# Attention values in one visit per step, three turned-weight banks, and the output-weight split on GpSimd

## The chip, the cores and the metric

The kernel runs on one core of a Trainium2 chip. The metric is the device time of one execution in microseconds (us), as the median of repeated runs. Beside it there is one profiled execution, whose trace all rows below come from.

## The reference

One inference step of a one-layer encoder, all in fp32. 1024 prompt tokens and 64 sample tokens (which also see a cache of 2048 positions) go through RMSNorm and one input projection of 3072 columns, then through two mixers side by side, an output matrix, a SwiGLU block and a final norm.

```python
qd, kd, vd, qs, ks_, vs = _project(n, w_in[l])
# differential attention: 4 heads, two 64-wide maps each, values 128 wide
p = softmax(where(visible, q.k/8 - slope*dist, -1e30))
a = p[:, :, 0] - lam * p[:, :, 1];  o = a @ v
# stick-breaking attention: 8 heads of 64, strictly causal
z = q.k/8;  log_keep = where(causal, log_sigmoid(-z), 0)
a = where(causal, exp(log_sigmoid(z) + cumsum_from_the_right(log_keep) - log_keep), 0);  o = a @ v
hp = xp + concat(od, osb) @ w_out[l]
y = rms_norm(hp + swiglu(hp, ...))
```

## The kernel before

The program goes through the projection, then `attend` (both attentions), then `mix` (the output matrix), then the feed-forward block. The change is in `attend` alone.

**Steps.** `attend` has 8 units (`NU`): 4 differential heads (`ND`), then 4 pairs of stick-breaking heads. A unit has 5 steps (`SPU`): four prompt steps of two query blocks each (1152 key columns together, for two maps or two heads), and one sample step of 2112 columns. So there are 40 steps; 0 to 19 are differential, 20 to 39 (`SB0` on) stick-breaking.

**One iteration, written by hand.** All engines run the same loop over iterations -3 to 40 and each iteration has three slices (`SLICES`, slots 0 and 1, slots 2 and 3, slot 4). In iteration i, slice by slice, TensorE does:

- `turn`: it transposes groups of the finished weights z of step i (3 groups for a differential prompt step, 5 for the others) into a bank of `ps_aT` (L1776);
- `values`: it multiplies turned weights, copied by ScalarE from `ps_aT` to `aT` (`collect`, L1445), with the values into `ps_o` (L1802, L1809, L1805);
- `score`: the products q.k of step i+3, up to 512 columns a unit, into the ring of four banks `ps_z` (L1743 to L1760);
- `prepare`: transposes of raw keys for the next unit, also through the ring (L1722). ScalarE and VectorE split them into a high and a low part (L1397, L1524).

A score or a prepare waits in `release` until the bank that it takes has been read. In the differential half VectorE reads the scores (`read_scores`, L1575) and ScalarE then takes the exponentials (`exps`, L1419); VectorE joins the two maps (`combine`, L1602). In the stick-breaking half ScalarE reads the scores with a sigmoid (`keep`, L1431 and L1436) and VectorE runs a scan over them (`survive`, L1619). A differential prompt score takes two banks a unit, one for each map; a sample score takes one.

**Where values stand.** `LAG` is 2. A differential step's group has its values at the slot of the group two places further on, so a prompt step has one group in the second slice of its own iteration and two in the first slice of the next. A stick-breaking step up to 37 (`gathered`) has four groups in the third slice of its own iteration and the fifth in that of the next. `ps_aT` has 2 banks, `ps_o` 2, `aT` 6 places.

**The output matrix's split.** VectorE splits w_out into a rounded high part (`split_w_out`, L1642) and the rest (`low_w_out`, L1649), 16 pieces of 128x512, at the ends of iterations 21 to 36. SyncE loads the pieces into the ring of six raw places `staging`, which the raw keys and values use too, in one fixed order, and waits for the release of the piece six places before. GpSimd multiplies `lowest` by a slope once per differential step (L1355), builds the masks, and is then idle until `mix`.

## Time and profile before

| what | value |
|---|---|
| median of 3 runs | 1408.41 us (1406.29 to 1408.46) |
| profiled execution | 1405.33 us, of which the span is 1403.5 us |
| TensorE busy | 1357.6 us, 97% |
| VectorE busy | 998.1 us, 71% |
| ScalarE busy | 620.5 us, 44% |
| GpSimd busy | 453.8 us, 32% |
| `attend` | from about 277 us to 575.9 us |
| iterations 20 to 39 of it | 434.9 us to the last scan's end, 571.8 us |

Busy time counts an instruction from its start to its end, with any time that it stands still in between. Matmuls overlap, so TensorE's gaps are best seen at its weight loads (PEld): each matmul has one, and "[0.29 <-X]" behind a row is the time that the engine stood idle before it and what ended that.

### The profile page before, as it was taken

Reading aid. Unit: us, or ns where it says so; the run is one execution under the profiler, and the core shown is the slowest. Engines: PE = TensorE matmul, PEld = TensorE weight load, DVE = VectorE, ACT = ScalarE, POOL = GpSimd, SP = SyncE. Lnnn points to the kernel's source line nnn. Section 1 sums busy time; section 2 is a strip of 40 time slices with the busy share of each in tenths; the row PEclk is TensorE's granted clock in tenths of the full one; section 3 lists DMA queues with packets and bytes.
Section 4 is the critical chain, followed back from the end, with each engine's and each line's share of the span. In section 5 each row is a group of like instructions: output and inputs, shape, how many; then the busy total and the mean of one; then the engine's idle time right before and its main releaser. Section 6 shows DMA issues by size and latency. Waiting matters only on the chain.

```text
span 1403.5 us, 23797 instructions
## 1 busy us (share of the span) xinstructions
PE 1357.6 (97%) x9152; PEld 1194.3 (85%) x9152; DVE 998.1 (71%) x1317; ACT 620.5 (44%) x1112; POOL 453.8 (32%) x416
## 2 busy tenths in 40 slices
PE   6999999989999999999799999999999999999997
PEld 5778888768888787788689999999999998788886
DVE  5896858698868999766686766565766666753466
ACT  6634333278887877333342132232132233533343
POOL 2133331200010000111274454454454454644354
PEclk9999999999999999999999999999999999999999
DMA  7265542465444555433134443444443448855554
GB/s 250 76 213 187 204 160 74 145 174 142 129 128 116 143 140 144 149 136 108 54 121 154 165 156 109 145 145 153 167 154 110 147 173 288 298 175 165 164 181 172
DMA packets 172200, 218.05 MB, mean 155 GB/s; under 512 B 19836, under 2 KB 110328, under 8 KB 170680
## 3 DMA queue, kind: packets, MB, share of 16 engines
q1 hardware_dynamic: 163416, 193.13, 42.5%
q0 software_dynamic: 3840, 12.58, 2.8%
q10 hardware_dynamic: 4832, 10.82, 2.1%
q8 instruction: 74, 1.21, 0.4%
q14 instruction: 38, 0.31, 0.1%
HBM read 152.98 MB, written 63.50 MB: 154 GB/s over the span
## 4 chain that ended last, share of the span: by engine, by line
PE 47%; DVE 1%; DMA 1%; issue 1%; ACT 0%; SPq 0%; POOL 0%; ACTq 0%; DVEq 0%
PE ps_feed L2997 11%; PE ps_feed L2998 11%; PE ps_feed L2999 11%; PE ps_feed L3028 4%; PE ps_feed L3027 4%; PE ps_feed L3026 4%; PE ps_feed L3042 1%; PE ps_feed L3043 1%; DMA aux<-in_w_down 1%; DMA aux<-t_dram 0%; DVE parts_early L2865 0%; DVE shared L2865 0%; DVE blocks L2843 0%; DVE blocks L2844 0%; DVE blocks L2910 0%
## 5 line engine op out<-in xcount | busy, mean ns | idle before, releaser
L792 PE MATMUL ps_proj<-shared 128*128 128x512 f32 x224 | 90.1, 402 | 2.1 <-DVE shared L546 1.2
L2678 ACT COPY aux<-ps_feed 128x544 f32<-128x544 f32 x22 | 13.5, 615 | 170.3 <-PE ps_feed L2999 170.3
L1445 ACT COPY aT<-ps_aT 128x512 f32<-128x512 f32 (+2 forms) x168 | 81.4, 528 | 16.7 <-PE ps_aT L1776 16.2
L793 PE MATMUL ps_proj<-shared 128*128 128x512 f32 x224 | 88.3, 394 | 0.0
L794 PE MATMUL ps_proj<-shared 128*128 128x512 f32 x224 | 88.1, 393 | 0.0
L2628 POOL TENSOR_TENSOR ring_more<-staging,ring_more 128x512 fp32r<-128x512 f32 x45 | 69.6, 1550 | 56.5 <-ACT ring_more L2664 56.3
L2628 POOL TENSOR_TENSOR shared<-staging,shared 128x512 fp32r<-128x512 f32 x41 | 60.0, 1468 | 83.4 <-ACT shared L2664 83.4
L1776 PE MATMUL ps_aT<-ident,z 128*128 128x128 f32 (+1 forms) x568 | 82.7, 279 | 3.4 <-DVE z L1619 2.1
L2892 DVE TENSOR_TENSOR blocks<-ps_feed,blocks 128x512 f32<-128x512 f32 x56 | 36.0, 682 | 66.2 <-PE ps_feed L3028 66.2
L1619 DVE TENSOR_TENSOR_SCAN z<-z,near 128x1024 f32<-128x1024 f32 (+7 forms) x64 | 81.4, 1334 | 0.0
L2997 PE MATMUL ps_feed<-shared,ring_more 128*128 128x272 f32 x264 | 76.6, 290 | 1.8 <-issue 1.8
L2997 PE MATMUL ps_feed<-parts_early,shared 128*128 128x272 f32 x256 | 74.5, 291 | 2.7 <-PEq L3184 2.7
L2999 PE MATMUL ps_feed<-shared,ring_more 128*128 128x272 f32 x264 | 76.2, 289 | 0.0
L1776 PEld LDWEIGHTS ps_aT<-ident,z 128*128 128x128 f32 (+1 forms) x568 | 63.3, 141 | 15.1 <-issue 7.4
L2998 PE MATMUL ps_feed<-shared 128*128 128x272 f32 x264 | 76.1, 288 | 0.0
L2998 PE MATMUL ps_feed<-parts_early,ring_more 128*128 128x272 f32 x264 | 76.1, 288 | 0.0
L2999 PE MATMUL ps_feed<-shared 128*128 128x272 f32 x264 | 76.1, 288 | 0.0
L2998 PE MATMUL ps_feed<-shared,ring_more 128*128 128x272 f32 x264 | 76.1, 288 | 0.0
L2999 PE MATMUL ps_feed<-parts_early,ring_more 128*128 128x272 f32 x264 | 76.0, 288 | 0.0
L2997 PE MATMUL ps_feed<-parts_early,ring_more 128*128 128x272 f32 x264 | 76.0, 288 | 0.0
L2997 PE MATMUL ps_feed<-shared 128*128 128x272 f32 x264 | 75.6, 286 | 0.0
L2998 PE MATMUL ps_feed<-parts_early,shared 128*128 128x272 f32 x256 | 74.6, 291 | 0.0
(372 smaller groups left out, 4520.3 us busy)
## 6 DMA issues: line engine op xcount, KB each, us to landing
staging<-s_dram SPq DMA_DIRECT2D x50, 256.0 KB, 4.4
staging<-in_w_gate SPq DMA_DIRECT2D x11, 1024.0 KB, 7.8
blocks<-in_w_up SPq DMA_DIRECT2D x11, 1024.0 KB, 5.4
blocks<-in_w_down SPq DMA_DIRECT2D x11, 1024.0 KB, 9.8
t_dram<-blocks SPq DMA_DIRECT2D x11, 1024.0 KB, 3.9
s_dram<-blocks SPq DMA_DIRECT2D x11, 1024.0 KB, 5.2
w_raw<-in_w_in SPq DMA_DIRECT2D x10, 1024.0 KB, 6.6
staging<-in_cache_sb_v POOLq DMA_DIRECT2D x31, 256.0 KB, 3.2
```

The source lines that it names most:

```text
L792: nc.tensor.matmul(res, a_hi[:, k, cols], b_hi[:, k], start=start, stop=False)
L793: nc.tensor.matmul(res, a_hi[:, k, cols], b_lo[:, k], start=False, stop=False)
L794: return nc.tensor.matmul(res, a_lo[:, k, cols], b_hi[:, k], start=False, stop=(k == HK - 1))
L1445: last = nc.scalar.copy(aT[:, G % AT, 0:f], ps_aT[:, G % 2, 0:f])
L1619: nc.vector.tensor_tensor_scan(back, back, mask[:, ::-1], 1.0, ALU.mult, ALU.max).then_inc(ready, 1)
L1776: last = nc.tensor.transpose(ps_aT[0:m, G % 2, k], z(x, at, m), t["ident"][:, :])
L2628: nc.gpsimd.tensor_tensor(w_lo, product_source(m)[0], w_hi.bitcast(F32), ALU.subtract).then_inc(w_lo_done, 1)
L2997: nc.tensor.matmul(res, w_hi[:, k], x_hi, start=(k == 0), stop=False)
L2998: nc.tensor.matmul(res, w_hi[:, k], x_lo, start=False, stop=False)
L2999: last = nc.tensor.matmul(res, w_lo[:, k], x_hi, start=False, stop=(k == HK - 1))
L3026: nc.tensor.matmul(res, a_hi[:, rows], b_hi, start=(k == 0), stop=False)
L3027: nc.tensor.matmul(res, a_hi[:, rows], b_lo, start=False, stop=False)
```

## The change

1. **Values in one visit.** Every step but the last has all its values in the first slice of the next iteration, behind the turns of slots 0 and 1 and ahead of the scores. ScalarE moves `output` of the step before to the second slice, behind the collects (and, in the differential half, behind the exponentials of that slice).
2. **Banks.** `ps_aT` gets a third bank, `ps_o` keeps one, `aT` gets a seventh place. A turn waits for the copy three groups back, and the values of step x wait for the output of step x-1.
3. **w_out on GpSimd.** The 16 casts and 16 subtractions move from VectorE's iterations to GpSimd's queue, behind the masks and ahead of its part of `mix`. Each waits only for its piece's load, and the ninth for the scores of step 34. `pad` shrinks by 512 columns a row.

```diff
-    RAW, RING, ZS, AT, LAG, POS = 6, 4, 4, 6, 2, 5
+    RAW, RING, ZS, AT, LAG, POS, TURNED = 6, 4, 4, 7, 2, 5, 3
...
     def gathered(x):
-        return SB0 <= x < NSTEP - 2
+        return x < NSTEP - 1
...
             if gathered(x):
-                at = (x, 2) if g < len(groups(x)) - 1 else (x + 1, 2 if gathered(x + 1) else 0)
-                values_at.setdefault(at, []).append(grp0[x] + g)
+                values_at.setdefault((x + 1, 0), []).append(grp0[x] + g)
             else:
-                y, j = owner[grp0[x] + g + LAG] if grp0[x] + g + LAG < len(owner) else (NSTEP, grp0[x] + g + LAG - len(owner))
-                values_at.setdefault((y, [j in slots for slots in SLICES].index(True)), []).append(grp0[x] + g)
+                values_at.setdefault((x, 2) if g < len(groups(x)) - LAG else (x + 1, 0), []).append(grp0[x] + g)
...
-        pad = sbuf("pad", [P, 768])
+        pad = sbuf("pad", [P, 256])
...
-        ps_aT = psum("ps_aT", [P, 2, 4, P])
-        ps_o = psum("ps_o", [P, 2, BANK])
+        ps_aT = psum("ps_aT", [P, TURNED, 4, P])
+        ps_o = psum("ps_o", [P, BANK])
...
@@ gpsimd @@
+            def split_w_out(n):
+                k, j = divmod(n, 2)
+                e = raw_of["wout", n]
+                part = (slice(None), slice(j * BANK, (j + 1) * BANK))
+                piece = raw[:, slot_of(e)].rearrange("p a b -> p (a b)")
+                if n == EARLY:
+                    pool.wait_ge(scored, seg0[SPU * (NU - 1)])
+                pool.wait_ge(raw_loaded[slot_of(e)], raw_landed[e])
+                nc.gpsimd.tensor_copy(t["wo_hi"][k][part], piece).then_inc(wo_hi_done, 1)
+                pool.wait_ge(wo_hi_done, n + 1)
+                nc.gpsimd.tensor_tensor(t["wo_lo"][k][part], piece, t["wo_hi"][k][part].bitcast(F32),
+                                        ALU.subtract).then_inc(wo_lo_done, 1)
...
             make_masks()
+            for n in range(2 * KD):
+                split_w_out(n)
             norm_heads_pool(nc, pool, t, 0)
...
@@ scalar @@
-                    if 0 <= i - 1 and s == 0 and not gathered(i):
+                    if 0 <= i - 1 and s == (1 if gathered(i) else 0):
                         output(i - 1)
...
-                    if s == 2 and gathered(i) and i - 1 >= 0:
-                        output(i - 1)
...
@@ vector: split_w_out and low_w_out go, and @@
-                for n in wout_at.get(i, ()):
-                    split_w_out(n)
-                for n in wout_at.get(i, ()):
-                    low_w_out(n)
...
@@ tensor @@
-                if G >= 2:
-                    pe.wait_ge(a_copied, G - 1)
+                if G >= TURNED:
+                    pe.wait_ge(a_copied, G - TURNED + 1)
...
-                    if x >= 2:
-                        pe.wait_ge(o_done, x - 1)
+                    if x >= 1:
+                        pe.wait_ge(o_done, x)
```

## Rows read from the trace of the kernel before

**Rows 1.** The page, part 1: busy us (share of the span) xinstructions.

```profile
PE 1357.6 (97%) x9152; PEld 1194.3 (85%) x9152; DVE 998.1 (71%) x1317; ACT 620.5 (44%) x1112; POOL 453.8 (32%) x416
```

**Rows 2.** Busy time by stretch; length, then each engine's busy us (instructions), clock, DMA.

```profile
300.00:350.00 50.00, 49.80 (x403) 43.60 (x403) 44.44 (x134) 43.06 (x104) 2.27 (x8) 1.00 0.54 151
...
537.80:571.80 34.00, 31.23 (x360) 25.60 (x360) 34.00 (x39) 22.00 (x48) 0.00 (x0) 1.00 0.34 98
sum 136.90, PE 131.68 PEld 108.17 DVE 127.11 ACT 103.66 POOL 0.00; mean PE 26.34 PEld 21.63 DVE 25.42 ACT 20.73 POOL 0.00
```

**Rows 3.** Timeline, differential half, TensorE's weight loads and VectorE: start, length, instruction.

```profile
332.75 0.08 DVE L1575 DVE_READ_ACCUMULATOR2_ANT lowest<- 128x1 f32 x1
332.95 0.21 PEld L1756 LDWEIGHTS ps_z<-kT_hi,qT_hi 64*128 64x128 f32 x2 [0.29 <-DVE lowest L1575]
...
336.99 1.15 DVE L1602 SCALAR_TENSOR_TENSOR z<-z,ratio 128x896 f32<-128x896 f32 x1
...
343.31 0.18 PEld L1756 LDWEIGHTS ps_z<-shared 64*128 64x128 f32 x2
...
344.44 0.69 DVE L1575 CUSTOM_DVE_ANT_0 z<-ps_z,near 128x512 f32<-128x512 f32 x1
...
344.90 0.31 PEld L1776 LDWEIGHTS ps_aT<-ident,z 128*128 128x128 f32 x3 [0.37 <-issue]
...
345.18 0.75 PEld L1802 LDWEIGHTS ps_o<-v,aT 128*128 128x128 f32 x6
...
345.67 0.08 DVE L1575 DVE_READ_ACCUMULATOR2_ANT lowest<- 128x1 f32 x1
...
346.05 0.19 PEld L1756 LDWEIGHTS ps_z<-shared 64*128 64x128 f32 x2
...
347.01 0.08 DVE L1575 DVE_READ_ACCUMULATOR2_ANT lowest<- 128x1 f32 x1
...
347.21 0.42 PEld L1722 LDWEIGHTS ps_z<-ident,staging 128*128 128x128 f32 x4 [0.19 <-issue]
```

**Rows 4.** Timeline, stick-breaking half, TensorE's weight loads.

```profile
444.24 1.94 PEld L1809 LDWEIGHTS ps_o<-aT,v 128*64 128x64 f32 x36 [0.17 <-ACT aT L1445]
...
446.36 0.42 PEld L1722 LDWEIGHTS ps_z<-ident,staging 128*128 128x128 f32 x4 [0.17 <-issue]
...
479.45 0.21 PEld L1756 LDWEIGHTS ps_z<-kT_hi,qT_hi 64*128 64x128 f32 x2 [1.03 <-issue]
...
560.06 0.86 PEld L1776 LDWEIGHTS ps_aT<-ident,z 128*128 128x128 f32 x8 [1.13 <-DVE z L1619]
```

**Rows 5.** Busy time of L1642 by stretch, the casts of the output matrix.

```profile
434.90:537.80 102.90, 3.34 (x8) 1.00 0.56 154
537.80:571.80 34.00, 2.99 (x8) 1.00 0.34 98
```

**Rows 6.** The same view of L1649, the subtractions.

```profile
434.90:537.80 102.90, 5.54 (x8) 1.00 0.56 154
537.80:571.80 34.00, 5.13 (x8) 1.00 0.34 98
```

**Rows 7.** Groups by line and shape: the longest prompt scan.

```profile
L1619 DVE TENSOR_TENSOR_SCAN z<-z,near 128x1024 f32<-128x1024 f32 x8 | 17.9, 2274 | 0.0
```

**Rows 8.** One line of GpSimd in the feed-forward block: ns, minimum, median and maximum.

```profile
L2628 POOL TENSOR_TENSOR shared<-blocks,shared x23: 1290/1301/3470, 713.4 to 1147.1; 128x512 fp32r<-128x512 f32 x23
```

**Rows 9.** Timeline, GpSimd beside VectorE, with two SBUF inputs at L1534 and L2844.

```profile
327.61 0.69 DVE L1534 SCALAR_TENSOR_TENSOR shared<-staging,shared 128x512 fp32r<-128x512 f32 x1
...
327.85 0.51 POOL L1355 TENSOR_SCALAR lowest<-lowest 128x8 f32<-128x8 f32 x1 [7.07 <-DVE lowest L1575]
...
342.37 0.20 POOL L1355 TENSOR_SCALAR lowest<-lowest 128x8 f32<-128x8 f32 x1 [6.38 <-DVE lowest L1575]
...
745.67 3.13 POOL L2628 TENSOR_TENSOR shared<-staging,shared 128x512 fp32r<-128x512 f32 x2 [7.89 <-ACT shared L2664]
...
745.86 1.78 DVE L2844 TENSOR_TENSOR blocks<-blocks 128x512 f32<-128x512 f32 x1
```

More of the change, by code:

```diff
@@ L1444, in collect @@
                 f = sum(m == P for _, _, _, _, m in bl)
-                last = nc.scalar.copy(aT[:, G % AT, 0:f], ps_aT[:, G % 2, 0:f])
+                last = nc.scalar.copy(aT[:, G % AT, 0:f], ps_aT[:, G % TURNED, 0:f])
                 if f < len(bl):
                     m = bl[f][4]
-                    last = nc.scalar.copy(aT[0:m, G % AT, f], ps_aT[0:m, G % 2, f])
+                    last = nc.scalar.copy(aT[0:m, G % AT, f], ps_aT[0:m, G % TURNED, f])
                 last.then_inc(a_copied, 1)
@@ L1457, in output @@
                     act.wait_ge(v_last_loaded[u % 2], 32 * ((u - ND) // 2 + 1))
-                o, ps = o_sb[:, x % 4], ps_o[:, x % 2]
+                o, ps = o_sb[:, x % 4], ps_o
                 if is_sample(x) and is_diff(x):
@@ L1634, in shift @@
                     nc.vector.tensor_tensor(cur, raw[0:rows, slot_of(e), 0], cur, ALU.subtract).then_inc(shifted, 1)
-            def split_w_out(n):
-                k, j = divmod(n, 2)
-                e = raw_of["wout", n]
-                if n == EARLY:
-                    dve.wait_ge(scored, seg0[SPU * (NU - 1)])
-                dve.wait_ge(raw_loaded[slot_of(e)], raw_landed[e])
-                nc.vector.tensor_copy(t["wo_hi"][k][:, j * BANK:(j + 1) * BANK],
-                                      raw[:, slot_of(e)].rearrange("p a b -> p (a b)")).then_inc(wo_hi_done, 1)
-            def low_w_out(n):
-                k, j = divmod(n, 2)
-                part = (slice(None), slice(j * BANK, (j + 1) * BANK))
-                dve.wait_ge(wo_hi_done, n + 1)
-                nc.vector.tensor_tensor(t["wo_lo"][k][part], raw[:, slot_of(raw_of["wout", n])].rearrange("p a b -> p (a b)"),
-                                        t["wo_hi"][k][part].bitcast(F32), ALU.subtract).then_inc(wo_lo_done, 1)
             def negative_lambda():
@@ L1772, in turn @@
                     pe.wait_ge(ready, ready0[x] + 2 * r + h + 1)
-                if G >= 2:
-                    pe.wait_ge(a_copied, G - 1)
+                if G >= TURNED:
+                    pe.wait_ge(a_copied, G - TURNED + 1)
                 for k, (_, _, _, at, m) in enumerate(groups(x)[g]):
-                    last = nc.tensor.transpose(ps_aT[0:m, G % 2, k], z(x, at, m), t["ident"][:, :])
+                    last = nc.tensor.transpose(ps_aT[0:m, G % TURNED, k], z(x, at, m), t["ident"][:, :])
                 last.then_inc(a_turned, 1)
@@ L1799, in values @@
                     val = v[u % 2][0:m, (NB if is_sample(x) else 0) + k]
-                    out = ps_o[:, x % 2]
+                    out = ps_o
                     if is_diff(x):
```

## The prediction

> **What bounds the kernel now.** I read the page first. TensorE is busy 97% of the span [rows 1], so a gain must come from time in which TensorE stands still or drains, not from lighter work elsewhere. Then the stretches of `attend`. In the differential half VectorE is busy 44.4 of 50 us and ScalarE 43.1 beside TensorE's 49.8 [rows 2]: three engines that are nearly full, so the order in which they hand over counts. In the stick-breaking half, 434.9 to 571.8 us, VectorE is busy 127.1 of 136.9 us, and from 537.8 on for all 34.0 us [rows 2]. There TensorE is the one that waits, for scans, as in the 1.13 us at 560.06 [rows 4]. So the stick-breaking half is bound by TensorE up to about 537 us, with VectorE 9.8 us short of full, and by VectorE behind it. What comes after `attend` is not touched.
>
> **Part 1a, values in the differential half.** No matmul goes away. What counts is what the moved one covered. In the iteration shown, the scores begin at 343.31, the turn of the third group stands at 344.90, the values of one group at 345.18, the third score unit at 346.05, and the second prepare at 347.21 [rows 3]. The third unit needs the banks of the first, which VectorE frees with its second read. That read's last instruction begins at 345.67. From the iteration before one sees what the hand-over takes: it begins at 332.75 and the waiting score at 332.95, 0.20 us later [rows 3]. So the bank is free at 345.87. The prepare at 347.21 is just such a wait: 347.01 plus 0.20 [rows 3]. From the first score to the second prepare this is a chain of VectorE's reads, 3.90 us long, and the 0.75 us of values inside it [rows 3] were free. After the change they stand ahead of the first score, and the chain behind it stays nearly as long. The turn ends at 345.21, a change of tile costs 0.17 us [rows 4], so the third unit could start at 345.38 but gets its bank at 345.87.
>
> The price by kind of iteration. In this kind the values cost 0.75 less 0.19, since VectorE starts its reads at 344.44 [rows 3], some 0.2 us later than the scores allow, and would start them on time: 0.55 us. Where VectorE is idle ahead of the reads I take the wait alone, 0.57 us. Where the bank was late already (332.95, 0.29 us of which 0.16 more than normal [rows 3]) it is 0.67. The two kinds left, with more turns between or the longer values or the longer join ahead of the reads (the 1.15 us from 336.99 [rows 3]), cost nothing: VectorE is behind by more than 0.4 us there and the later scores only meet it. Iterations 1 to 16 hold three of each of the first three kinds: 3 x (0.55 + 0.57 + 0.67) = 5.4 us. Iteration 0 has the same gap as the last kind, and 17 to 19 change over to ScalarE's reads with a filler less: 1.1 us together. Sum **+6.5 us**. Bounds: if ScalarE and VectorE use the time to catch up, +2; if each of 17 iterations loses its 0.75 us, +13. I take the middle, nearest to the iteration that the rows show.
>
> **Part 1b, values in the stick-breaking half.** Here values use another tile shape (128*64), and each change of shape shows a gap of 0.17 us: before the values at 444.24, before the prepare at 446.36 [rows 4]. An iteration now has six such changes (turns to scores, scores to turns, and so on round the values). With values between turns and scores it has five, where the fifth group is followed by a prepare or a turn. About 14 iterations up to 537 us gain 0.2 us: 2.8 us; the last two steps, whose values alternate with turns, gain about 1.4.
>
> **Part 2, banks.** The third bank takes away the wait of the fifth group for its copy, some 0.45 us once and less elsewhere. The second score unit waits now for banks that the prepare of the iteration before took; the worst has 1.03 us of idle time at 479.45 [rows 4], and there are four, 2.3 us over the normal gap. With 2 us of values ahead of them they have their banks. Sum of 1b and 2 up to 537 us: 2.8 + 0.4 + 2.3 = 5.5 us. The single `ps_o` costs nothing: `output` of x-1 stands in the second slice of iteration x and the values of x in the next iteration, with the prepares between. If ScalarE were late by more than that, each step would wait; it is busy 43.1 of 50 us [rows 2], so I keep 0 to +3 for it. The later `output` in the differential half delays stores that nobody waits for.
>
> **Part 3, VectorE's relief.** It loses 3.34 + 2.99 + 5.54 + 5.13 = 17.0 us [rows 5, 6], so 110.1 us of work are left of 127.1. 8.1 of the 17.0 lie in the full last stretch.
>
> **Part 3, GpSimd's load.** Sixteen subtractions take 1.29 us each when nothing disturbs them [rows 8], and this is off the path. But the two engines stand in each other's way. The VectorE instruction with both inputs in SBUF at 745.86 takes 1.78 us [rows 9], where the same size takes 10.67/16 = 0.67 us [rows 6]: it waited 1.10 us for the GpSimd instruction that had begun at 745.67. A small GpSimd instruction with one input takes 0.20 us, and 0.51 us when VectorE's two-input instruction at 327.61 runs beside it [rows 9], up to whose end it waits. So whichever starts first keeps the other out, one input or two. A scan has both inputs in SBUF and up to 2.27 us [rows 7]; scans follow on each other without a gap, and at each seam a waiting GpSimd instruction gets in. A subtraction costs VectorE 1.10 us. The cast on GpSimd isn't in the trace: not under the 0.20 of the small one, not over 1.10; I take 0.55, as it has one input for the subtraction's two. If all 32 hit a scan: 16 x 1.65 = 26.4 us. About a fifth of VectorE's time goes to instructions that read PSUM, or is idle, so I take 21.8. The rule behind it stands in the Trainium skill, GPSIMD Engine Reference, section Key points: GpSimd shares its SBUF interfaces with VectorE, in contention with VectorE instructions of two SBUF inputs. The trace agrees (1.78 against 0.67 us). No row shows a scan beside GpSimd; if the rule holds for it in full, rival B is what comes. The same page, section Elementwise, gives about 1.03 cycles an element at 1.2 GHz for simple bodies, an estimated 0.44 us for the cast; with it the 26.4 would be 24.6.
>
> GpSimd's pieces come in as loads land, so the second half of the splits falls again behind 530 us, where VectorE is full. VectorE then has 110.1 + 21.8 = 131.9 us of work, and some 5 of its 9.8 idle us stay, since it still waits for ScalarE's casts: **136.9 us, as long as now**. TensorE's 5.5 us are not paid out, because VectorE has become the bound. Tail: -0.4 us.
>
> **Sum**: 6.5 + 0 - 0.4 = +6 us on the profiled execution's 1405.33 us (span 1403.5 and 1.8 around it). That is 3.1 us under the median 1408.41, so I forecast 1414.5 us. Same means within 0.2%, 2.8 us, about what a measurement of this kernel can tell.
>
> **Rivals.**
> - **A, the forecast**, +3 to +9 us: chance 0.37.
> - **B, the scans are kept out in full** and the idle time stays: 110.1 + 26.4 + 5 = 141.5, +4.6 us in the second half, with 6.5 about +11 us, 1419.5. For it: no gap between scans, and GpSimd always has work once pieces have landed. Against: while pieces are on their way nothing collides. Chance 0.17.
> - **C, faster.** The scan takes 2.2 ns a column (2.27 us for 1024 [rows 7]) where a plain instruction takes 1.3 (0.67 us for 512), so it may leave GpSimd room, and the 32 instructions cost VectorE under 8 us. Then TensorE is the bound: it gains 5.5 up to 537 us, the scan waits of about 4 behind it, 1.4 of shape changes and 0.4: 11 us. With +6.5 from the first half that is -5, 1403.5; with the low end +2 it is -9, 1399.5. It decides from the point at which blocking is below some 12 us. For it: no scan beside GpSimd is in the trace. Against: each two-input instruction that is. Chance 0.28.
> - **D, it cancels**: about half the blocking, 12 to 16 us, lets the second half pay back the 6.5. 1408.5 within 2.8. Chance 0.18.
>
> Faster 0.28, same 0.18, slower 0.54. Range 1401 to 1423, from C's main case to a little above B; A's own is 1411.5 to 1417.5.
>
> **What the changed profile would show.** The period of differential iterations grows by about 1.8 us for five (GpSimd's L1355 marks them); the third score unit stands idle 0.4 to 0.9 us for L1575. L1619 has maxima 1.1 us over the clean length, and GpSimd's subtractions reach 3 us. TensorE's waits at 479.45 are gone. The last scan ends as far behind the first as now. Wrong would be: differential iterations of the old period, or scans of unchanged length beside GpSimd.

## The result and the profile after

The changed kernel takes 1421.15 us (median of five, 1419.02 to 1422.51), against 1408.41 before: ratio 1.0098, 95% interval 1.0085 to 1.0112 (over pairs of runs; the two medians alone give 1.0090). That is +12.7 us where +6 was forecast: the right side and inside the range, but twice the size. The profiled execution took 1419.02 us with a span of 1417.1, against 1405.33 and 1403.5. Three executions further below (3418 us in `filler_two_outputs` and in `late_pieces`, 1590 us in `drained_seams`) stood far off the others of the same kernel, and the medians and intervals leave them out.

The page of the changed kernel, part 1, answers to [rows 1]:

```profile
PE 1357.8 (96%) x9152; PEld 1196.5 (84%) x9152; DVE 999.4 (71%) x1285; ACT 616.5 (44%) x1112; POOL 515.9 (36%) x448
```

TensorE has the same work and stands still longer. VectorE gave up 32 instructions, 17.0 us of work, and is yet 1.3 us busier than before. The same kernel with that work left on VectorE (`split_on_vector` below) has it busy 1002.4 us, only 3.0 more: some 14 of the 17.0 came back as time in which VectorE's instructions stand blocked beside GpSimd's. GpSimd has 32 more, and 62 us more busy time.

Busy time by stretch: the differential one of [rows 2], then the stick-breaking half from its first scan to the end of its last, after and before.

```profile
300.00:350.00 50.00, 47.05 (x374) 40.29 (x373) 41.80 (x125) 40.20 (x100) 1.75 (x7) 1.00 0.50 139
...
sum 145.66, PE 136.60 PEld 117.17 DVE 134.26 ACT 104.76 POOL 58.11; mean PE 68.30 PEld 58.58 DVE 67.13 ACT 52.38 POOL 29.05
```
```profile
sum 147.24, PE 142.02 PEld 117.67 DVE 135.87 ACT 110.37 POOL 0.00; mean PE 71.01 PEld 58.84 DVE 67.93 ACT 55.19 POOL 0.00
```

So the differential half has lost the fullness that [rows 2] showed (TensorE 47.05 of 50 us instead of 49.80), and the stick-breaking half is 1.6 us shorter. Four marks put the loss in its places.

| us from the start | before | after | difference |
|---|---|---|---|
| GpSimd's last scaling of `lowest` | 409.23 | 417.09 | +7.9 |
| first scan | 424.63 | 434.00 | +9.4 |
| end of the last scan | 571.87 | 579.66 | +7.8 |
| first product of `mix` | 575.92 | 589.20 | +13.3 |

First half +9.4, second half -1.6, hand-over to `mix` +5.5 (4.05 us before, 9.54 after).

**The first half.** What TensorE's weight loads waited for from 277 to 575 us, in total, number, longest:

```profile
PEld ps_z L1747 <- DVE lowest L1586: 15.9, 17, 3.1
PEld ps_aT L1767 <- DVE z L1630: 10.4, 8, 2.3
```

Before, the first of these was 7.3 us in 8 waits and the second 3.3 in 6. The four waits for it in one period of five iterations, from the timeline:

```profile
348.53 0.21 PEld L1747 LDWEIGHTS ps_z<-shared 64*128 64x128 f32 x2 [0.67 <-DVE lowest L1586]
...
355.26 0.22 PEld L1747 LDWEIGHTS ps_z<-shared 64*128 64x128 f32 x2 [0.74 <-DVE lowest L1586]
...
362.22 0.21 PEld L1747 LDWEIGHTS ps_z<-shared 64*128 64x128 f32 x2 [0.50 <-DVE lowest L1586]
...
371.12 0.22 PEld L1747 LDWEIGHTS ps_z<-shared 64*128 64x128 f32 x2 [1.00 <-DVE lowest L1586]
```

Each is the third score unit, where the values of [rows 3] used to stand. The sum is 2.91 us; before, that kind of wait stood once in a period, at 0.30. The period grew from 33.4 to 36.1 us.

**The granted clock.** Up to GpSimd's last scaling the loss is 7.9 us, and 9.4 at the first scan. The 1.5 us between the two lie in a stretch in which TensorE was granted half its clock (start and end, length, busy time of PE, PEld, DVE, ACT and POOL, granted clock, share of DMA, GB/s):

```profile
420.00:423.50 3.50, 1.57 (x14) 1.18 (x14) 0.00 (x0) 3.49 (x6) 1.56 (x3) 1.00 0.86 202
423.50:426.90 3.40, 3.40 (x18) 3.40 (x17) 1.52 (x4) 2.43 (x6) 0.00 (x0) 0.50 0.54 131
426.90:430.00 3.10, 2.98 (x28) 2.48 (x26) 0.00 (x0) 0.82 (x2) 0.00 (x0) 1.00 0.61 178
570.30:573.70 3.40, 3.40 (x29) 3.07 (x29) 3.40 (x3) 1.17 (x2) 3.40 (x1) 0.50 0.10 19
```

In the second row 0.50 is the lower level, 1.2 GHz. There the weight loads of 18 values take 2.90 us instead of 2.09, those of 6 turns 1.30 instead of 0.69 and those of 8 prepares 1.05 instead of 0.86: 1.6 us more in all. TensorE had been busy 1.57 of the 3.5 us ahead of it. The kernel before was busy 1.60 of 3.5 us at the same work (412.0 to 415.5) and kept the full clock, as it did from 297.6 to 693 us, so why the clock fell here and not there stays open. The fourth row is a second such stretch, after TensorE had stood still 2.29 us for a scan of 2112 columns (the far scan of step 37, below); the values and turns in it take 1.5 us more.

**The hand-over.** GpSimd's last four instructions of the split (start, length):

```profile
563.52 1.54 POOL L1382 CAST shared<-staging 128x512 fp32r<-128x512 f32 x1
565.14 15.59 POOL L1384 TENSOR_TENSOR shared<-staging,shared 128x512 fp32r<-128x512 f32 x1
580.68 0.60 POOL L1382 CAST shared<-staging 128x512 fp32r<-128x512 f32 x1
581.36 1.27 POOL L1384 TENSOR_TENSOR shared<-staging,shared 128x512 fp32r<-128x512 f32 x1
```

and VectorE beside them:

```profile
564.58 0.62 DVE L1645 TENSOR_TENSOR v<-staging,v 64x128 f32<-64x128 f32 x1
565.13 4.54 DVE L1630 TENSOR_TENSOR_SCAN z<-z,far 128x2112 f32<-128x2112 f32 x1
569.60 10.06 DVE L1630 TENSOR_TENSOR_SCAN z<-z,near 128x896 f32<-128x896 f32 x8
```

The subtraction needs 1.27 us and lasted 15.59: it started 0.01 us after the far scan of step 37 and ended only when eight more scans were through. None of the nine scans was delayed. The raw place of that piece is where the first mixed tokens are loaded, and SyncE issued that load right behind the subtraction's end (start, length, queue, line):

```profile
580.81 0.32 SPq L880 DMA_DIRECT2D staging<-mixed  x1
```
```profile
565.31 0.32 SPq L880 DMA_DIRECT2D staging<-mixed  x1
```

The second of these rows is before's. `mix` begins with the squares of these tokens, which now found VectorE idle for 6.55 us:

```profile
586.21 0.69 DVE L903 TENSOR_TENSOR staging<-staging 128x512 f32<-128x512 f32 x1 [6.55 <-DMA staging<-mixedT]
```

### The profile page after: what moved, and what is told of

It reads as the page before. It is cut to its first block, busy times and chain, and to the rows that moved or that the text cites. A ratio compares the mean times of both kernels' runs of the same rounds, so it can differ in the third digit from the quotient of the medians.

```text
span 1417.1 us, 23796 instructions
## 1 busy us (share of the span) xinstructions
PE 1357.8 (96%) x9152; PEld 1196.5 (84%) x9152; DVE 999.4 (71%) x1285; ACT 616.5 (44%) x1112; POOL 515.9 (36%) x448
## 4 chain that ended last, share of the span: by engine, by line
PE 47%; DMA 1%; DVE 1%; issue 1%; SPq 0%; ACT 0%; POOL 0%; ACTq 0%; DVEq 0%
PE ps_feed L2988 11%; PE ps_feed L2989 11%; PE ps_feed L2990 11%; PE ps_feed L3019 4%; PE ps_feed L3018 4%; PE ps_feed L3017 4%; PE ps_feed L3033 1%; PE ps_feed L3034 1%; DMA aux<-in_w_down 1%; DMA aux<-t_dram 0%; DVE parts_early L2856 0%; DVE blocks L2834 0%; DVE blocks L2835 0%; POOL shared L2624 0%; DVE blocks L2901 0%
## 5 line engine op out<-in xcount | busy, mean ns | idle before, releaser
L1630 DVE TENSOR_TENSOR_SCAN z<-z,near 128x1024 f32<-128x1024 f32 (+7 forms) x64 | 91.1, 1484 | 0.0
L1767 PEld LDWEIGHTS ps_aT<-ident,z 128*128 128x128 f32 (+1 forms) x568 | 63.9, 142 | 20.0 <-DVE z L1630 10.4
```

What stands on the lines that cost most here:

```text
L1630: nc.vector.tensor_tensor_scan(back, back, mask[:, ::-1], 1.0, ALU.mult, ALU.max).then_inc(ready, 1)
L1767: last = nc.tensor.transpose(ps_aT[0:m, G % TURNED, k], z(x, at, m), t["ident"][:, :])
```

## The experiments

Each was run beside the kernel before, whose median there was 1406.0 to 1407.5 us. "Hand-over" is from the last scan's end to the first product of `mix`, "second half" from the first scan to the last scan's end.

**1. diff_as_before.** The old differential half under the new stick-breaking half, with the old banks:

```diff
-        return x < NSTEP - 1
+        return SB0 <= x < NSTEP - 1
-        ps_aT = psum("ps_aT", [P, TURNED, 4, P])
-        ps_o = psum("ps_o", [P, BANK])
+        ps_aT = psum("ps_aT", [P, 2, 4, P])
+        ps_o = psum("ps_o", [P, 2, BANK])
```

> The changed kernel, but the differential steps keep their values and outputs where they were, with two turned-weight and two output banks. Theory (the chain of score reads lost its filler, and the last GpSimd pieces hold back the mixed loads): the period of differential iterations is that of before, 33.4 us for five; the second half and the hand-over stay as in the changed kernel: 5 us over before, 1413.5. Rival (GpSimd's share of the work costs everything, the first half is only in passing): 11 us or more over before.

Measured: 1420.56 us, ratio 1.0102 [1.0087, 1.0117]. The period is 33.4 again and the first scan at 426.7, so the first half's loss does come from its own part of the change. But the total did not fall, since the second half took 156.2 us; the hand-over took 9.1 us. With two banks a turn waits for ScalarE's copy, once the values no longer stand between turns:

```profile
PEld ps_aT L1770 <- issue: 18.0, 27, 1.4
```

It was not the clean isolation that I meant it to be. It shows that the one visit needs the third bank.

**2. split_on_vector.** The changed kernel with the 16 casts and subtractions back in VectorE's iterations.

> The changed kernel with the output matrix split on VectorE as before. Theory: the first half keeps its +7.8 us; the hand-over from the last scan to the first product of mix goes back from 8.7 to some 4.1 us; the second half is freed from blocked scans and loses about what VectorE gets back: 5 to 8 us over before, 1413.5 to 1416.5. Rival (GpSimd costs everything): equal to before or faster.

Measured: 1415.20 us, 1.0068 [1.0053, 1.0083]; hand-over 5.1 us; second half 144.8 us, no longer than with GpSimd's help (145.7). The hand-over came as forecast. The time is 8.8 us over before, where 5 to 8 was said, and no stretch below full clock is left at the far scan. This is the cleanest comparison for Part 3: of the 13.3 us up to the first product of `mix`, 4.4 go away in the hand-over when VectorE has the split back, and 0.9 in the half.

**3. split_alone.** The kernel before with the split on GpSimd and nothing else changed.

> The kernel before with the output matrix split on GpSimd, nothing else. Theory: first half as before; the second half about as before, the hand-over +4.5 us: 4 to 7 us over before. Rival (the share of GpSimd is harmless, only the order of values costs): within 1 us of before or faster by up to 8.

Measured: 1412.80 us, 1.0049 [1.0032, 1.0065]. The last scan ends 2.3 us earlier than before (569.5), and the hand-over is 10.35 us instead of 4.1, with the same picture:

```profile
554.99 15.60 POOL L1386 TENSOR_TENSOR shared<-staging,shared 128x512 fp32r<-128x512 f32 x1
```

Part 3 of the change alone costs 6.4 us between the profiled executions, all of it behind the last scan. 3.9 of them stand before the first product of `mix` (579.87 against 575.92). Behind it TensorE was at half its clock up to 584.9 us, which takes a part of the rest.

**4. filler_back.** The changed kernel with the values of a differential step in the second slice of the next iteration, between VectorE's reads, in one visit.

```diff
-                values_at.setdefault((x + 1, 0), []).append(grp0[x] + g)
+                values_at.setdefault((x + 1, 1 if is_diff(x) else 0), []).append(grp0[x] + g)
```

> The changed kernel, but the values of differential steps stand in the second slice of the next iteration, behind the turn of the third group and ahead of the third score unit, all in one visit; their output in the third slice. Theory: with 2.1 us of values inside the chain of reads the wait of the third unit is gone and the period for five is 33.4 us or less: 7.8 us under the changed kernel, 1413.5. Rival (one output bank or the later output costs the time): still 36 us for five, as the changed kernel or slower.

Measured: 1419.53 us, 1.0095 [1.0080, 1.0110]. The waits for `lowest` fell from 15.9 us to 6.9, as they should, but the period only to 34.9: TensorE now waits for VectorE's key splits behind the long visit (`shared` 3.7 us, `kT_lo` 2.9). Half a miss: the visit of 2 us is too long where 0.75 us stood.

**5. diff_visit_alone.** The kernel before with only the differential values in one visit, all banks and everything else as before.

```diff
+            elif is_diff(x):
+                values_at.setdefault((x + 1, 0), []).append(grp0[x] + g)
```

> The kernel before with one edit: the values of the differential steps stand in one visit in the first slice of the next iteration and their output in the second slice; two banks for turned weights and two for output stay, the stick-breaking half and the split stay as before. If the place of the values is what costs the first half: a period of about 36.2 us for five iterations instead of 33.4, the first scan 8 to 9 us later than before (433), and +7 to +9 us in all. If the single output bank or the third turned bank has a part in it: a period clearly under 36.2. My forecast of this term was +6.5 in all, a period of 35.2.

Measured: 1420.69 us, 1.0092 [1.0077, 1.0107]. The period is 37.4 us, more than the changed kernel's 36.1, and the first scan is 13.4 us late. The waits for `lowest` are exactly those of the changed kernel, and turns wait for copies on top:

```profile
PEld ps_z L1758 <- DVE lowest L1577: 15.9, 17, 3.1
PEld ps_aT L1778 <- issue: 6.7, 9, 1.6
```

So the place of the values alone costs 13.4 us at the first scan, and the new banks give 4 of it back. Both this 13.4 and the changed kernel's 9.4 hold about 1.6 us of half clock (here from 426.6 us on).

**6. sb_visit_three_banks.** The kernel before with the stick-breaking values in one visit, and three banks for turned weights and one for output throughout.

> The kernel before with the values of the stick-breaking steps in one visit, three banks for turned weights and one for output; the differential half keeps its order of values and VectorE keeps the split of w_out. My forecast of parts 1b and 2 was a TensorE that is 5.5 us earlier at 537 us, not paid out while VectorE is the bound. Theory: scans ready earlier, so from the first scan to the last scan's end some 144 to 147 us instead of 147.2 and an end of 1403 to 1408. Rival, that the third bank is only what mends the visit's own loss: 147 to 150 us and 1408 to 1412. The single output bank may add 0 to 3 us in the differential half, where a visit in the second slice now waits for the output of the step before.

Measured: 1411.25 us, 1.0029 [1.0018, 1.0040]. The second half takes 144.1 us, 3.1 less than before. The first half, with its old order of values, has a period of 35.2: a visit in the second slice waits for the single output bank.

```profile
PEld ps_o L1801 <- issue: 8.0, 14, 1.0
```

**7. filler_two_outputs**, and once more for its profile. `filler_back` with the four banks shared out by half of the program: two and two in the differential half, three and one in the other.

> The kernel of the run filler_back with two banks for turned weights and two for output in the differential half, three and one in the stick-breaking half. filler_back put the values of a differential step back between VectorE's two reads and still had a period of 34.9 us; the run with only the stick-breaking half changed had 35.2 with the single output bank. If the single output bank is what filler_back still lacked: a period of 33.4 to 33.8, the first scan at 425 to 427 instead of 431.8, and 4 to 6 us under filler_back's time (1414 to 1415). If something else in the place of the values (one visit instead of two) costs it: a period of 34.5 or more.

> The kernel of the run filler_two_outputs once more for its profile, since the profiled execution of that run was disturbed; its time was 1420.73 us, no less than filler_back's. If the single output bank was what filler_back lacked: a period of 33.4 to 33.8 us and a loss elsewhere. If the one visit between VectorE's reads costs by itself: a period of 34.5 or more, with waits of the turns for the copies or for the reads behind them.

Measured: 1419.41 us, 1.0092 [1.0074, 1.0110], then 1418.42 in a single run, with a period of 34.9 us as in `filler_back`, and the same waits (`shared` 3.3 us, `kT_lo` 2.9). The output bank was not what `filler_back` lacked. The single visit is.

**8. last_four_on_vector.** `split_alone` with pieces 12 to 15 on VectorE as before.

```diff
-            for n in range(2 * KD):
+            for n in range(12):
                 split_w_out(n)
```

> The kernel before with pieces 0 to 11 of w_out split on GpSimd and the last four on VectorE as before. With all sixteen on GpSimd the last scan ended 2.3 us earlier than before, but the hand-over to mix took 10.3 us instead of 4.1. If that hand-over is due only to GpSimd being kept out beside the last scans: a hand-over of about 4 to 5 us, a last scan 1 to 2 us earlier than before and a time 1 to 2 us under before. Rival: the gain of the relief comes from the last four pieces alone, then the time is that of before within 1 us.

Measured: 1406.89 us, 0.9997 [0.9988, 1.0007]. The hand-over is 4.55 us, so the loss of 6 us is gone. The last scan ends at 571.5 instead of 571.9: the 2.3 us that `split_alone` had gained went with the last four pieces, as the rival said. There GpSimd had done piece 12 beside the scans and held the subtraction of 13 to their end, and did 14 and 15 behind them, so VectorE was rid of their work inside the half.

**9. banks_by_half.** The kernel before, with the stick-breaking values in one visit and the banks shared out by half:

```diff
+    def turned_bank(G):
+        g0 = grp0[SB0]
+        return G % 2 if G < g0 else (G - g0 + g0 % 2) % 3
+
+    def output_bank(x):
+        return 2 + x % 2 if x < SB0 else 3
...
-        ps_aT = psum("ps_aT", [P, 2, 4, P])
-        ps_o = psum("ps_o", [P, 2, BANK])
+        ps_x = psum("ps_x", [P, 4, BANK])
```

> The same four banks are shared out by half: in the differential half two for turned weights and two for output, with the order of values as before; in the stick-breaking half three and one, with the values in one visit. VectorE keeps the split. If the two earlier runs add up (first scan at 424.6 as before, 144.1 us from the first scan to the last scan's end, a hand-over of 4 to 5 us): mix starts near 573.5 instead of 575.9 and the time is about 2.5 us under before, ratio 0.998. Rival: the shorter stick-breaking half was only slack caught up after a late start (there the first scan was 10 us late and VectorE waited for nothing at first); then 147 us again and the time of before.

Measured: 1405.63 us (11 runs), 0.9990 [0.9981, 0.9998]. Period 33.4, second half 144.1 us, hand-over 5.1. This is the best version, 1.5 us under before, which is within what I called no change. The first half is as before here, so the short second half is no catching up after a late start. TensorE has its full clock through all of `attend`.

**10. banks_by_half_mixed.** The same with pieces 0 to 13 split on GpSimd.

> The same with pieces 0 to 13 of w_out split on GpSimd and the last two on VectorE, so that no GpSimd instruction of the split is left when the far scan of step 37 starts. If VectorE's relief counts wherever VectorE is the bound: 2 to 3 us less than with the split on VectorE, so about 4 to 5 us under before, ratio 0.997. If blocking eats the relief: within 1 us of the run with the split on VectorE. If a piece is still held out: a hand-over of about 9 us and a time above before.

Measured: 1408.14 us, 1.0007 [0.9998, 1.0016]. No piece was held at the end, yet the second half is 146.9 us instead of 144.1: in the good arrangement the help of GpSimd costs more than it brings. The relief theory missed. About half of the 2.8 us is the clock: from 562.2 to 565.7 us TensorE was granted 0.51, and one visit of values took 3.14 us instead of 1.95.

**11. by_half_old_end.** `banks_by_half` with the last two steps in their old order.

> The kernel of the run banks_by_half, but the last two steps keep the order of values of the kernel before (turns and values in turn). banks_by_half had its last scan end 2.3 us earlier than before and lost 1.1 of it in the hand-over (5.1 us against 4.1). If that is due to the changed order of the last two steps: the hand-over is 4.1 again and the time 1 us less, 2 to 3 us under before, ratio 0.998 to 0.9985. If the hand-over is set by the mixed loads, which count from the last outputs, it stays at 5 and the time is that of banks_by_half, ratio 0.999.

Measured: 1405.82 us, 0.9994 [0.9986, 1.0003]; the time is that of the second expectation, but the hand-over came as in neither: it grew to 6.8 us, with TensorE itself busy in it. So the 1.1 us that the new order costs there (5.14 against 4.05) has no shown cause.

**Why GpSimd is held out.** Five runs on the changed kernel.

**12. seams.** A memset of 128x1 on VectorE behind each scan from step 36 on.

> The changed kernel with a memset of 128x1 on VectorE behind each scan of steps 36 to 39, each to a column of its own that nobody reads. If GpSimd is kept out only because scans follow each other with no other VectorE instruction between them: no GpSimd subtraction over 4 us, a hand-over of 4 to 5 us instead of 9.5, and a time 3 to 5 us under the changed kernel's 1421. If the seam makes no difference (VectorE keeps the memory as long as its queue holds scans that are ready): a subtraction of about 15 us again and the same time, plus under 1.5 us for the memsets.

Measured: 1420.32 us, 1.0101 [1.0079, 1.0124]. The memset, 0.06 us long, starts 0.01 us behind the start of the scan ahead of it, runs beside it and opens nothing. The hand-over is 9.0 us. This time it was the cast that fell beside the far scan:

```profile
566.55 15.30 POOL L1382 CAST shared<-staging 128x512 fp32r<-128x512 f32 x1
```

**13. drained_seams.** VectorE waits for its own scan to end, then writes the memset, for every scan from step 37 on.

> The changed kernel in which, from step 37 on, VectorE waits for each of its own scans to have ended and then writes a memset of 128x1 before the next scan, so that there is a true gap between scans. If GpSimd is kept out because the queued scans leave no gap: the longest GpSimd instruction under 6 us, and a hand-over of 4 to 6 us instead of 9.5. If it is kept out in spite of a gap: about 15 us again.

Measured: 1418.73 us, 1.0090 [1.0071, 1.0108]; longest GpSimd instruction 5.60 us (the far scan and its own 1.3), hand-over 4.6. The true gaps let GpSimd in. The time cannot be told from the changed kernel's (the intervals overlap): the hand-over is 5 us shorter, and from the first scan to the first product of `mix`, which holds the gaps too, 152.5 us against 155.2.

**14. late_pieces**, and once more for its profile. GpSimd starts its last two pieces only behind the first of the eight scans.

> The changed kernel in which GpSimd starts its last two pieces only when the first scan behind the far scan of step 37 has ended. If the far scan is what keeps it out: it gets in at the seams of the following eight scans, no instruction over 4 us, and a hand-over of about 5 us. If it is the row of scans with nothing between them: the cast that begins behind the first of them is held until the last scan's end, some 8 to 9 us, and the hand-over is 10 us or more, as all four instructions are left over.

> The kernel of the run late_pieces once more, since the profiled execution of that run was disturbed. If the far scan is what keeps GpSimd out: it gets in at the seams of the following eight scans, no instruction over 4 us. If it is the row of scans behind it: the cast that begins behind the first of them is held until the last scan's end, some 8 to 9 us.

Measured: 1423.12 us, 1.0113 [1.0098, 1.0129], and 1418.74 in a single run, with a hand-over of 9.1 us. With the far scan long over, the cast is held through the seven scans that are left:

```profile
572.11 8.42 POOL L1384 CAST shared<-staging 128x512 fp32r<-128x512 f32 x1 [7.71 <-DVE z L1632]
```

So the far scan is not needed for the hold.

**15. one_gap.** A single gap, behind the far scan; the eight scans follow each other as ever.

```diff
+                if is_sample(x) and x > NSTEP - 5:
+                    dve.wait_ge(ready, ready0[x] + j + 1)
+                    nc.vector.memset(pad[:, 0:1], 0.0)
```

> The changed kernel in which VectorE waits for its far scan of step 37 to have ended, once, and writes a memset of 128x1 before the row of eight scans. If one true gap lets exactly the waiting instruction in: GpSimd's fifteenth subtraction lasts about 5.6 us as in drained_seams, and the next cast is held until the last scan's end, some 9 to 10 us; hand-over 9 to 10 us as in the changed kernel. If the long hold needs the far scan: the next instructions get in at the seams and the hand-over is 4 to 5 us.

Measured: 1418.64 us, 1.0087 [1.0066, 1.0109], hand-over 4.85. The first expectation held for the subtraction (5.60 us) and missed what follows. The outcome is that of the second, though its premise, that the far scan is needed for the hold, was ruled out by `late_pieces_again`. The waiting subtraction got in at the gap, and the two instructions behind it got in at seams that have no gap:

```profile
565.34 5.60 POOL L1384 TENSOR_TENSOR shared<-staging,shared 128x512 fp32r<-128x512 f32 x1
570.89 2.34 POOL L1382 CAST shared<-staging 128x512 fp32r<-128x512 f32 x1
573.30 2.86 POOL L1384 TENSOR_TENSOR shared<-staging,shared 128x512 fp32r<-128x512 f32 x1
```
```profile
569.91 2.91 DVE L1630 TENSOR_TENSOR_SCAN z<-z,near 128x896 f32<-128x896 f32 x1
572.74 2.36 DVE L1630 TENSOR_TENSOR_SCAN z<-z,near 128x896 f32<-128x896 f32 x1
```

These scans take 1.99 us undisturbed. The first lasted 2.91, as it had to wait for the subtraction, and at its end the cast got in. The second waited for the cast, and at its end the next subtraction got in. That gave the theory for the last run.

**16. far_waits.** No gap. The far scan only waits for the fifteenth cast, so that it starts beside a subtraction that has begun.

```diff
+                if is_sample(x) and x > NSTEP - 5:
+                    dve.wait_ge(wo_hi_done, 15)
                 back = z(x, at, n)[:, ::-1]
```

> The changed kernel in which the far scan of step 37 waits until GpSimd has ended its fifteenth cast, so that the subtraction behind that cast has begun and the far scan has to wait for it. Theory: a scan that had to wait for GpSimd lets GpSimd in at its end, and one that started free is followed by the next scan without a seam. In one_gap this held through the rest of the row. Then there is no long hold here, although no gap is added: the far scan lasts about 5.7 us instead of 4.54, the sixteenth cast is held about 5 us and gets in at the far scan's end, its subtraction under 3.5 us, the hand-over is 4 to 5 us and the time 2 to 3 us under the changed kernel's. Rival: it was the gap that helped in one_gap; then the sixteenth cast is held some 15 us, and the time is that of the changed kernel plus 1.

Measured: 1419.76 us, 1.0080 [1.0057, 1.0103]. The lengths came as forecast, far scan first:

```profile
567.10 5.67 DVE L1632 TENSOR_TENSOR_SCAN z<-z,far 128x2112 f32<-128x2112 f32 x1
```
```profile
568.30 4.87 POOL L1382 CAST shared<-staging 128x512 fp32r<-128x512 f32 x1
573.25 2.86 POOL L1384 TENSOR_TENSOR shared<-staging,shared 128x512 fp32r<-128x512 f32 x1
```

The hold is gone without a gap. The hand-over is 7.0 us, not the 4 to 5 forecast. TensorE is still at the last steps' values behind the last scan, and at half its clock (after it had stood still 3.46 us for the far scan):

```profile
571.80:578.60 6.80, 5.78 (x44) 5.28 (x44) 6.80 (x5) 1.17 (x2) 4.23 (x2) 0.50 0.05 12
```

One visit of values in it takes 3.71 us instead of 1.95 and the turns 1.57 instead of 0.86, some 2.5 us. The time was forecast 2 to 3 us under the changed kernel's; the intervals of the two overlap, so that is not shown.

## Why the prediction had the side right and the size wrong

**Part 1a, the differential half: +6.5 forecast, +9.4 measured.** The mechanism was right, and its own mark came: the third score unit stands idle 0.50 to 1.00 us for VectorE's second read, where 0.4 to 0.9 was said, and the period grew. It grew by 2.7 us, where the forecast had 1.8. The three kinds that it gave a price came near it: 0.67 for 0.55 (at 348.53), 0.74 for 0.57 (at 355.26), and from 0.30 to 1.00 for the 0.67 of the late bank (at 371.12). The step that failed is "the two kinds left" that "cost nothing". One of them does, that of the sample step. The other has a new wait of 0.50 us at 362.22. I had argued that VectorE is behind by more than 0.4 us there and the later scores only meet it. They do not: ahead of that iteration's first read VectorE stood idle 0.18 us before the change, for ScalarE, and stands idle 0.87 us after it, for the score. Before and after:

```profile
356.86 0.69 DVE L1575 CUSTOM_DVE_ANT_0 z<-ps_z,near 128x512 f32<-128x512 f32 x1 [0.18 <-ACT z L1419]
```
```profile
360.79 0.69 DVE L1586 CUSTOM_DVE_ANT_0 z<-ps_z,near 128x512 f32<-128x512 f32 x1 [0.87 <-PE ps_z L1751]
```

Over the first half this makes 7.9 us up to GpSimd's last scaling. The rest of the 9.4 is the stretch at half clock, for which the forecast had no term.

The bound of +13, "if each of 17 iterations loses its 0.75 us", is met in number by the +13.4 of `diff_visit_alone`, but by luck. There the waits for VectorE's reads are those of the changed kernel, 15.9 us against 7.3 before, and the rest is turns that wait for copies (6.7 us against 2.1) and the half clock. In a period the four waits grew by 2.6 us, not by five times 0.75.

**Part 2, banks: 0 for the first half, 0.4 + 2.3 for the second.** In the first half I gave the third bank no value: with values no longer between the turns it is worth 4 us (13.4 against 9.4). In the second it carries the visit: 156.2 us with two banks, against 145.7 in the changed kernel with three. That the single `ps_o` "costs nothing" held in the changed kernel, where the values stand behind the output (0.5 us of waits for it). It costs 1.8 us a period under the old order, which was not the question. TensorE's waits at 479.45 are gone, as forecast.

**Parts 1b and 3, the stick-breaking half: 0 forecast, -1.6 measured.** The forecast had two large terms that cancel, and so they do. The gaps before TensorE's turns, scores and prepares that the profile puts down to no other engine ("issue") fell in the half from 15.3 to 7.9 us, and its waits for scans grew from 3.3 to 10.4 us. So TensorE's gain was not paid out, as VectorE is the bound. The third bank and the one visit with VectorE's split left in place shorten the half by 3.1 us, so some of it is paid out when GpSimd keeps away. The blocking was over-priced. VectorE's busy time in the half is 136.6 us with the split on it (`split_on_vector`) and 134.3 with the split on GpSimd, so of 17.0 us of work given away some 14.6 came back there. The forecast had 21.8, for which its own "about a fifth" off 26.4 would be 21.1. Some 10 of the 14.6 lie on the near scans. Their groups, the longest and the shortest, answer to [rows 7]:

```profile
L1630 DVE TENSOR_TENSOR_SCAN z<-z,near 128x1024 f32<-128x1024 f32 x8 | 19.7, 2502 | 0.0
...
L1630 DVE TENSOR_TENSOR_SCAN z<-z,near 128x128 f32<-128x128 f32 x8 | 6.7, 877 | 0.0
```

The shortest took 396 ns before, and the longest scan of the form 128x1024 now takes 3.36 us where 2.26 is clean: the 1.10 us forecast. GpSimd's subtractions reach 3.14 us, where 3 was said. VectorE's idle time in the half is 11.4 us, as it was before (147.24 less 135.87), where the forecast took 4.8 off it; too much blocking and too little idle time nearly cancel. In Part 1b itself 14 shape changes of 0.17 us are 2.4 us, not 2.8.

**The tail: -0.4 forecast, +5.5 measured.** This is the largest error and the second step that failed. It rests on two sentences: that GpSimd's subtractions are "off the path", and that "at each seam a waiting GpSimd instruction gets in". The first overlooks the one place where they are on it: GpSimd's last pieces hold the raw place that the first mixed load needs, and the end of the half has no slack. The moved step should have been followed to SyncE's queue. The second is what the trace shows up to 565 us and not after. With the split back on VectorE the hand-over is 5.14 us, so 4.4 of the 5.5 are due to the split on GpSimd and 1.1 to the rest of the change. Measured from the first scan, the hold alone is worth about 3 us: 155.2 us to the first product of `mix` with it, 152.0 in `one_gap` and 152.5 in `drained_seams` without, and 149.9 with no split on GpSimd at all. "The last scan ends as far behind the first as now" missed by 1.6 us.

**The rivals.** B came closest in time (+11) and by the wrong mechanism, since scans were blocked less than forecast and the second half did not grow. Neither it nor the forecast had the hand-over. The sum of the terms as measured is 9.4 - 1.6 + 5.5 = 13.3 us, against 13.7 between the two profiled executions and 12.7 between the medians.

Nothing of the change is a gain in this form. What is good in it is the stick-breaking visit with three banks, 3.1 us in the half, and it is paid out only if the differential half keeps its order and its two output banks. Even then 1.1 us goes in the hand-over, and 1.5 of 1407 us is left.

## What to carry to other kernels

When work is moved to an engine "off the path", look for what its last piece releases, and put the last pieces on the engine that finishes them surely. Here twelve of sixteen moved at no cost under the old order of values, and the last four cost 6 us; under the new order fourteen cost 2.5 us.

Where a short burst of products stands between two reads that form a chain, price its removal in each kind of iteration from the rows, before you call one free: here four of five kinds paid 0.5 to 0.74 us for a burst of 0.75. Count on a freed bank or buffer only together with the order that needs it: two banks with the new order cost some 10 us in the second half, and one output bank with the old order 1.8 us a period in the first.

Where a change makes TensorE wait, look at its granted clock in the profile after as well: here 1.6 of the 9.4 us in the first half are work at half clock and not a wait.

## What the runs showed of the hardware

**Who gets in at a seam.** GpSimd's subtraction was held 15.6 us beside nine scans in four kernels (the changed one, `split_alone`, `filler_back`, `filler_two_outputs_again`), and its cast 15.3 us in `seams` and 15.1 in `diff_as_before`, though it had got in at every seam just before. In that last row of scans one rule fits: a VectorE scan that had itself waited for GpSimd let the next GpSimd instruction in at its end, and a scan that had started free was followed by the next scan with GpSimd still outside. `late_pieces_again` (no scan had waited: held for all seven), `one_gap` and `far_waits` (made to wait once: never held again) agree with it, and `far_waits` was forecast by it.

Outside that row it does not hold. In the changed kernel, and at the same place in seven others, a scan starts free and a cast gets in at its end all the same:

```profile
509.28 2.29 DVE L1630 TENSOR_TENSOR_SCAN z<-z,near 128x1024 f32<-128x1024 f32 x1
```
```profile
509.98 2.00 POOL L1382 CAST shared<-staging 128x512 fp32r<-128x512 f32 x1 [15.85 <-DMA staging<-in_w_out]
```
```profile
511.48 2.63 DVE L1630 TENSOR_TENSOR_SCAN z<-z,near 128x1024 f32<-128x1024 f32 x1
```

The first scan takes 2.27 us clean, so it had not waited; the cast was held to its end and ran, and the next scan, queued behind, took 2.63. Also, VectorE's 64x128 subtraction ahead of the far scan had itself waited for GpSimd in the changed kernel (0.62 us, against 0.25 in `late_pieces_again`, where GpSimd was idle), yet the far scan got in behind it. In `seams` the held cast starts 0.13 us before the far scan by the profile, so there the start does not decide it either. What decides who is next stays open.

The Trainium skill, SBUF — State Buffer, section SBUF: two separate sides, states that whichever of the two starts first has the shared ports for its whole instruction and the other blocks; the scan that was kept out 0.92 us agrees. The page does not say who is next when one of them always has an instruction ready, and that is where the 15.6 us come from.

**The cast.** An undisturbed 128x512 cast takes GpSimd 0.60 us, where I took 0.55. The estimate in the prediction from the Trainium skill, GPSIMD Engine Reference, section Elementwise, was 0.44 us; the measurement decides.
